# First weight load moved to ScalarE's DMA queue, and half of a layer's last LayerNorm statistics moved from VectorE to ScalarE

## The reference, cut to what matters

```
for i in range(2):
    h   = x @ w_in[i]                     # layer 0: 12 query heads, 3 key/value heads, 4 memory-query heads
    mix = attention(h) + cross-attention into 256 memory tokens
    x   = layer_norm(alpha * x + mix @ w_out[i])
    x   = layer_norm(alpha * x + moe(x))  # 64 experts, 8 a token, one shared expert

def layer_norm(x, g, b):
    mu  = mean(x); var = mean((x - mu)**2)
    return (x - mu) * rsqrt(var + 1e-5) * g + b
```

## Time and profile before

| | |
|---|---|
| median of 3 runs | 1244.28 us |
| profiled execution | 1245.44 us, its span 1243.7 us |
| TensorE busy | 95% of the span |
| VectorE, ScalarE, GpSimd busy | 30%, 23%, 4% |
| DMA | 359 GB/s over the span |
| mean granted TensorE clock | 0.995 |

### The profile page before, as it was taken

The page is one execution under the profiler, slowest core; times in us unless marked ns, Lnnn a source line. Parts: engine busy times, 40 slices in busy tenths (PEclk is TensorE's granted clock), DMA queues, the critical chain, the costliest instruction groups (busy, mean ns, idle before and its releaser), DMA issues.

```text
span 1243.7 us, 23026 instructions
## 1 busy us (share of the span) xinstructions
PE 1182.4 (95%) x9010; PEld 714.6 (57%) x9010; DVE 378.4 (30%) x977; ACT 288.0 (23%) x702; POOL 55.7 (4%) x99
## 2 busy tenths in 40 slices
PE   7999999999989999998999999999999899999994
PEld 6774755555555555554577747555555545555552
DVE  0333723122222222221523457222222222222215
ACT  1443312122121212221123333121222112121211
POOL 1232000000000000000002100000000000000000
PEclk9999999999999999999999999999999999999998
DMA  9425799999999999999960268999999999999994
GB/s 343 173 106 213 301 410 419 421 421 422 422 422 421 420 419 421 422 421 420 394 237 1 70 268 335 413 421 420 421 422 422 422 420 420 405 421 422 422 420 180
DMA packets 70965, 446.92 MB, mean 359 GB/s; under 512 B 6896, under 2 KB 10352, under 8 KB 20720
## 3 DMA queue, kind: packets, MB, share of 16 engines
q1 hardware_dynamic: 70464, 444.89, 87.2%
q10 hardware_dynamic: 432, 1.05, 0.2%
HBM read 444.86 MB, written 1.05 MB: 359 GB/s over the span
## 4 chain that ended last, share of the span: by engine, by line
issue 52%; PE 34%; DMA 7%; POOL 3%; DVE 3%; ACT 0%; SPq 0%; DVEq 0%; POOLq 0%
PE bank L1098 8%; PE bank L1088 8%; PE bank L1129 7%; DMA ring<-in_w_up 6%; PE bank L630 4%; PE bank L1137 2%; POOL soft L603 2%; PE bank L688 2%; PE bank L649 1%; PE bank L1105 1%; PE bank L972 1%; DMA ring<-in_w_in_a 1%; POOL work L603 1%; PE bank L994 1%; DVE work L1451 1%
## 5 line engine op out<-in xcount | busy, mean ns | idle before, releaser
L1098 PE MATMUL bank<-ring,work 128*64 128x256 f32 x1984 | 225.2, 379 | 12.4 <-DMA ring<-in_w_up 12.4
L1088 PE MATMUL bank<-ring,work 128*64 128x256 f32 x1984 | 227.7, 382 | 6.8 <-DMA ring<-in_w_gate 6.8
L1129 PE MATMUL bank<-ring,work 128*32 128x512 f32 x2032 | 233.0, 595 | 0.0
L1088 PEld LDWEIGHTS bank<-ring,work 128*64 128x64 f32 x1984 | 140.6, 137 | 115.3 <-issue 55.8
L1098 PEld LDWEIGHTS bank<-ring,work 128*64 128x64 f32 x1984 | 146.5, 137 | 82.6 <-issue 17.6
L1744 DVE TENSOR_TENSOR yhalf<-bank,yhalf 128x512 fp32r<-128x512 f32 x128 | 88.6, 692 | 210.4 <-ACT yhalf L1236 210.4
L1736 DVE SCALAR_TENSOR_TENSOR work<-work,gcol,bank 128x256 f32<-128x256 f32 x64 | 30.8, 481 | 361.1 <-issue 344.2
L1129 PEld LDWEIGHTS bank<-ring,work 128*32 128x32 f32 x2032 | 60.3, 109 | 126.9 <-issue 120.1
L1236 ACT ACTIVATE yhalf<-bank 128x512 fp32r<-128x512 f32 x128 | 76.4, 597 | 194.5 <-PE bank L1129 194.5
L1236 ACT ACTIVATE work<-bank 128x512 f32<-128x512 f32 (+4 forms) x181 | 79.5, 440 | 118.8 <-PE bank L630 40.7
L1236 ACT ACTIVATE back<-bank 128x128 fp32r<-128x128 bf16 x64 | 17.8, 278 | 288.6 <-PE bank L1061 288.6
(11 more groups left out here) (160 smaller groups left out, 814.7 us busy)
## 6 DMA issues: line engine op xcount, KB each, us to landing
ring<-in_w_down SPq DMA_DIRECT2D x127, 1024.0 KB, 15.2
ring<-in_w_gate SPq DMA_DIRECT2D x124, 1024.0 KB, 15.1
ring<-in_w_up SPq DMA_DIRECT2D x124, 1024.0 KB, 16.4
ring<-in_w_in_b SPq DMA_DIRECT2D x3, 3072.0 KB, 16.3
ring<-in_w_out SPq DMA_DIRECT2D x4, 2048.0 KB, 7.8
ring<-in_w_mem_kv SPq DMA_DIRECT2D x2, 2048.0 KB, 15.3
home<-in_w_gate SPq DMA_DIRECT2D x4, 1024.0 KB, 14.8
ring<-in_w_in_a SPq DMA_DIRECT2D x1, 3072.0 KB, 17.4
```

The costliest lines, as they stand in the source:

```text
L1088: last = pe.matmul(gate_bank[slots_of(e), 0:HID], xg[:, k, slots_of(2 * j + e)], w[e][0][:, k, :], start=(k == 0), stop=(k == KT - 1))
L1098: last = pe.matmul(up_bank[slots_of(e), 0:HID], xg[:, k, slots_of(2 * j + e)], w[e][1][:, k, :], start=(k == 0), stop=(k == KT - 1))
L1129: last = pe.matmul(yb[half][rows_of(t, e), :], hT[b][:, f, slots_of(e, t)], w[e][:, f, half * 512:half * 512 + 512], start=(f == 0), stop= ...
```

## The change

Three things are done.

1. Part 0 of `in1` is no longer issued by SyncE between tile 1 of `x` and `in0`, but by ScalarE as its very first instruction, ahead of `sinkrow`. SyncE's queue goes from `x` straight to `in0`.
2. In the last norm of each layer the statistics of tile 1 are taken by ScalarE. As soon as `x` holds all four sums it makes minus the mean, with a Copy over 1024 columns scaled by -1/1024 whose accumulator gives the row's sum (semaphore `mean_less`). Then comes the square root for tile 0, as before; then a Square over 1024 columns with minus the mean as bias, whose accumulator gives the sum of squared differences (semaphore `stats`); then a square root scaled by 1/1024. The elementwise results go to `passed`, a part of `work` that nobody reads then.
3. VectorE drops the two `bn_stats` and the `bn_aggr` of tile 1, and adds minus the mean where it subtracted the mean.

```
+        passed = work[:, 5120:6144]
...
             def load(it):
                 if it == (0, "in1"):
-                    load_part(it, 0)
                     return
...
+            dst, src = item_loads((0, "in1"))[0]
+            act.dma_start(dst, src).then_inc(sem("landed_in1_0_0"), 16)
             act.dma_start(sinkrow[:], sinks.broadcast_to([P, MIX_HEADS])).then_inc(sem("sinkrow"), 16)
...
-                for t in range(TT):
-                    norm_std(2 * l + 1, t)
+                act.wait_ge(sem(f"sums_read_{l}"), 4 * rounds + 1)
+                act.activation(passed, x[:, 1, :], ACT.Copy, scale=-1.0 / D, accum_out=mv[:, 1, 0:1]).then_inc(sem("mean_less"), 1)
+                norm_std(2 * l + 1, 0)
+                act.wait_ge(sem("mean_less"), l + 1)
+                act.activation(passed, x[:, 1, :], ACT.Square, bias=mv[:, 1, 0:1], accum_out=mv[:, 1, 1:2]).then_inc(sem("stats"), 1)
+                act.wait_ge(sem("stats"), TT * (2 * l + 1) + 2)
+                act.activation(std[:, 1, :], mv[:, 1, 1:2], ACT.Sqrt, scale=1.0 / D, bias=eps[:]).then_inc(sem("std"), 1)
...
-            def norm(n, src, t):
-
-                dve.bn_aggr(mv[:, t, :], stats[:, t, :, :]).then_inc(sem("stats"), 1)
+            def norm(n, src, t, less=False):
+
+                if not less:
+                    dve.bn_aggr(mv[:, t, :], stats[:, t, :, :]).then_inc(sem("stats"), 1)
...
-                                              op0=ALU.subtract, op1=ALU.mult))
+                                              op0=ALU.add if less else ALU.subtract, op1=ALU.mult))
...
-                for t in range(TT):
-                    for half in range(2):
-                        last = statistics(x, t, half)
-                    link(last)
-                    norm(2 * l + 1, x, t)
+                for half in range(2):
+                    last = statistics(x, 0, half)
+                link(last)
+                norm(2 * l + 1, x, 0)
+                dve.wait_ge(sem("mean_less"), l + 1)
+                norm(2 * l + 1, x, 1, less=True)
```

## The result

The changed kernel takes 1246.55 us, the median of 22 runs (1245.7 to 1248.5), beside 1244.71 us for the kernel before in as many (1242.6 to 1247.0). The ratio is 1.0017, with a 95% interval of 1.0011 to 1.0023: 1.8 to 2.1 us slower, between 1.4 and 2.9. Forecast were +3.05 us (a median of 1247.3, own range 1246.1 to 1248.8, that is +1.8 to +4.5), and a chance of 0.60 of being slower by more than 0.2%. The measured change lies at the lower edge of that range and just inside 0.2%. The profiled execution took 1246.58 us, its span 1244.8.

What follows compares the result with a forecast made beforehand. TensorE, busy 95% of the span, was taken to bound the kernel, so only its waits count. Start +4.4, clock +0.2 and end -1.55 gave +3.05 us: 1247.3 us on the median of 1244.28, own range 1246.1 to 1248.8.

Steps and rivals of the forecast that it cites:

- Where the loss comes from: Start: queues alternate packet by packet, `in1`'s small packets get the smaller half beside `in0`, delaying line 630 by 4.4 us.
- Rival A: Start: descriptors served in order of issue, `in1` lands at 10.4, line 630 1.65 us earlier, total 1241.1 us; chance 0.09.
- A2: Start: served in issue order, `in1` also ahead of tile 1 of `x`; line 630 at 13.0, total 1243.5 us; chance 0.09.
- B: Start: the slow first microseconds aren't `sinkrow`'s and stay; +1.6 us on the forecast, 1248.9 us; chance 0.11.
- the tail: Start: 1.1 us added to the reckoned transfer time to reach `in1`'s landing, taken from the kernel before.
- The clock: Start: TensorE's clock costs line 630 more after some 7 us idle instead of 2; +0.2 us, between 0 and +0.5.
- The shift goes through: Whole kernel: loads behind the start wait for TensorE's progress, so line 630's shift reaches the end in full.
- rival D: After the start: a later wait that doesn't move absorbs the delay, only the end counts; 1242.7 us; chance 0.04.
- The end: Layer 1's last norm: VectorE loses tile 1's statistics, ScalarE's work stays hidden; -1.55 us, range -1.6 to +0.1.
- rival C: Last norm: ScalarE comes late, by 2.1 us passes (1248.8) or idle time behind the table load (1248.3); chance 0.12.
- the landing's term: Start: `in1` lands at 16.5 instead of 12.02 us, line 630 starts at 16.7; +4.4 us, bounds +3.5 to +5.2.

Runs made afterwards that it cites:

- e5: Changed kernel, but SyncE issues `in0` only when part 0 of `in1` has landed: 1241.55 us, ratio 0.9969 to the kernel before.
- e6: Changed kernel, but `in0` issued as four column parts, with packets of 768 bytes instead of 3072: 1243.10 us, ratio 0.9983 to the kernel before.
- e3: Kernel before, with `sinkrow` taken off ScalarE's queue and issued by SyncE behind `in0`: 1243.81 us, ratio 0.9997 to the kernel before.
- e1: Kernel before with only the start's edit, part 0 of `in1` on ScalarE's queue: 1248.67 us, ratio 1.0038 to the kernel before.
- e12: Changed kernel, unchanged, profiled once more: one execution, 1247.51 us.
- e2: Kernel before with only the norm's edit, tile 1's statistics on ScalarE: 1243.53 us, ratio 0.9997 to the kernel before.
- e11: Kernel before, unchanged, profiled once more: one execution, 1245.07 us.
- e10: Changed kernel with 12 unread identity transposes on TensorE ahead of `x` and 60 behind it: 1244.72 us, ratio 1.0002 to the kernel before.
- e9: e5 with 12 unread identity transposes on TensorE ahead of `x` and 12 behind it: 1239.04 us, ratio 0.9956 to the kernel before.

## Why the prediction was right or wrong, point by point

**Where the loss comes from: right.** The queues take turns by count of packets beside `in0`, `in1`'s small packets get the smaller part of the bytes, and TensorE waits for it: e5 and e6 show it, each by one edit. Rival A (order of issue, a landing by 12 us) is out, so is A2 (tile 1 set nothing), and B: the slow first microseconds are `sinkrow`'s (e3), and the changed kernel doesn't have them.

**Its size: the bytes and the tail were mis-sized.** I had `in1` landing at 16.5 and line 630 at +4.4, between +3.5 and +5.2. (Those bounds were loose: they leave out the 0.24 us between landing and line 630, and half the tail would give +3.9, not +3.5.) Three profiles with this start (changed, e1, e12) have line 630 at 15.57, 15.34 and 15.94, mean 15.62; three of the old one (before, e2, e11) at 12.26, 12.21 and 12.21: +3.4, just under my lower bound. 0.3 us of the miss is the rate, 0.40 MB/us for 0.39. The rest one sees by counting packets of more than 512 bytes and under 2 KB, which are `in1`'s 1024. All that had moved by 11.6 us in the kernel before, and by 14.8 us in the changed one:

```profile
DMA packets 1560, 2.90 MB, mean 250 GB/s; under 512 B 192, under 2 KB 1216, under 8 KB 1560
...
DMA packets 2127, 4.87 MB, mean 329 GB/s; under 512 B 115, under 2 KB 1139, under 8 KB 2127
```

0.2 us earlier it was 1023 packets in both, with 2.81 and 4.79 MB in all. So before, some 0.2 MB of `in0` had already gone when the last packet of `in1` moved (2.62 MB is `x` and `in1` alone), and the landing came about 0.5 us behind it: my tail of 1.1 us was half bytes, half delay. In the changed kernel the last packet moved behind some 4.83 MB, not 4.98, and the landing came about 0.6 us behind it. That is 0.4 us less for the bytes and 0.5 less for the tail. One reason for the fewer bytes is visible too: by 6 us `in1`'s queue had moved 339 packets and `x`'s 226, where the forecast had them equal.

**The clock: the mechanism right, the term too small.** I had +0.2 us, up to +0.5. The 32 matmuls take 9.90 us on the mean of the three new starts and 9.30 on that of the three old ones: +0.6, a rough number from three and three, as the old ones alone differ by 1.5. With the waits filled they take 7.3 (e10). That the old start is slow too I had seen; what I had not is that its price differs so much between executions (8.7 to 10.2).

**The shift goes through: right.** From the start of line 649's stage to the first addition at the end of layer 0 it is 580.5 us in the kernel before (606.68 - 26.22; e11 the same) and 580.7 in the changed one (611.39 - 30.73; e12 the same); in thirteen of the fourteen profiles it lies between 580.4 and 581.0, in e10 it is 581.6. To the first addition of layer 1 it is 1201.4 to 1203.2 in all of them: 1203.2 and 1201.4 in the kernel before, 1201.4 and 1202.0 in the changed one. The first profile of the kernel before has the 1203.2: with its slow memory keys it is 17.2 us from that addition to the transposes at 623.91, where e11 has 15.2. So against that profile the changed kernel's shift of 4.5 us seems to have shrunk to 2.7 at the end. Nothing between gives a delay back; rival D is out, and the loss of e1 says so too.

**The end: right.** -1.55 forecast, -1.57 in the profile. The passes took 1.06 and 1.13 us for my 1.15, the root of tile 0 was 0.45 us early (1237.6 for 1238.05), the Square's result 0.7 us ahead of the subtraction. The load of the table is followed at once by the root, at 1237.31, with nothing like the drain of the Trainium skill (ScalarE: Activation LUTs, What ACT_TABLE_LOAD costs) between; the trace decides against it here, and rival C is out. At the end of layer 0 the saved time stayed hidden, as said: VectorE's part is shorter, but from the first addition to TensorE's first transpose of `x` it is 15.22 us in the changed kernel (626.61 - 611.39) and 15.24 in e11 (623.35 - 608.11).

**The sum.** With +3.4, +0.6 and -1.57 the runs' own terms give +2.4 us, inside the measured 1.4 to 2.9. The forecast of +3.05 had the right parts. The two at the start were off in opposite ways: the landing's term came out 1.0 us lower and the clock's 0.4 us higher. That they partly cancel is luck: with the clock's term as forecast the runs' terms would give +2.0. The most likely outcome given was over 1246.8 us, and the measured 1246.55 lies a little under that.

**The best version seen.** e5 is the change with one wait more, and 3.5 us faster than the kernel before; e9, with the transposes, 5.5 us, though that the transposes help there isn't shown.

## What to carry to other kernels

In this kernel a second DMA queue gave no more bandwidth, only another place in line: while both queues were full they moved like counts of packets, so the one with the larger packets got more of the bytes. Put the transfer that something waits for on a queue of its own only if nothing large is queued beside it until it has landed, and keep small packets (here 48 bytes) off a second queue while the first one matters. Where a microsecond or two decide, compare stages over several profiles and not one profile with one, and count what a wait does to TensorE's clock behind it as well as the wait.

## What the runs showed of the hardware that I had not expected

- 128 packets of 48 bytes on the other queue cost the first stage 0.6 MB in 4 us: 155 and 180 GB/s between 2 and 6 us against 281 and 357 without them (e3).
- The equal turns don't begin at once. From 4 to 5 us `in1`'s queue moved 206 packets and `x`'s only 23, and tile 1 of `x` came between 7.4 and 8.1 us; equal counts show beside `in0` (84 and 81, from 10 to 11 us).
- TensorE's granted clock was at its two levels, 1.2 and 2.4 GHz, at places that differ between executions of one kernel: at the memory keys of the kernel before it read 0.50 in the first profile (8.86 us) and 1.00 in e11 (7.17 us). At the start the first 32 matmuls alone moved line 649 from 26.22 to 27.64 us in the same kernel (8.72 and 10.20 us); the column reads 1.00 there, so that this is the clock too is inferred from their rate.
